# Latent attention in a two-block network: weight splits moved up, the query root finished on one engine, key roots by a power, rotary keys turned behind each latent norm

## The chip, the cores and the metric

The program runs on one core of a Trainium2 chip. The metric is the device time of one execution in microseconds (us): lower is better. The engines named below are TensorE (PE, with its weight loads as PEld), VectorE (DVE), ScalarE (ACT), GpSimd (POOL) and SyncE (SP), which here only issues transfers. Each runs its own instructions in order and meets the others at semaphores.

## The reference, cut to what matters

Two network blocks run one after the other on 256 tokens of width 1024. Their stages are called ffn0, mamba, ffn1, ffn2, mla and ffn3 (the first block), and conv and stick (the second). Only the latent attention (mla) is touched by the change:

```python
def mla_mixer(h, positions, w_in, q_a_norm, kv_a_norm, w_q_b, w_kv_b, q_norm, k_norm, w_out):
    proj = h @ w_in                                   # 1024 -> 384 + 256 + 32
    cq = rms_norm(proj[..., :384], q_a_norm)
    ckv = rms_norm(proj[..., 384:640], kv_a_norm)
    k_rope = proj[..., 640:]
    q = (cq @ w_q_b).reshape(b, s, 16, 96)            # 64 "nope" + 32 "rope" per head
    kv = (ckv @ w_kv_b).reshape(b, s, 16, 128)        # 64 key + 64 value per head
    ...
    q_nope, q_rope, k_nope, k_rope = (rms_norm of each, over its own last axis)
    q_rope = apply_rope(q_rope, cos, sin)
    k_rope = apply_rope(k_rope, cos, sin)
    o = causal_block_attention(q_nope, q_rope, k_nope, k_rope, v)
    return o.reshape(b, s, 1024) @ w_out
```

`rms_norm(x, w)` is `x * rsqrt(mean(x*x) + 1e-6) * w`.

## The kernel before, in words

**Products.** Every large product is done in fp32r as three matmuls (`product`, lines 559 to 561): high part times high part, high times low, low times high. So each weight unit (up to 2048 columns of 128 partitions, 1 MB) that lands in `raw` is split twice: ACT copies it, rounded, to `w_hi` (line 1173), and DVE subtracts to get `w_lo` (line 1668). Units go round a ring of four slots. SP may load unit u when `w_lo` of unit u-4 is done; ACT may split unit u when PE has used unit u-4; PE may use unit u when its `w_lo` is done.

**The order is written out by hand**, engine by engine. `split_to(n)` on ACT and on DVE means "split all units up to n, here in the queue". An engine's queue is in order, so whatever stands behind a split waits for it.

**The mla stage** has twelve weight units, called W0 to W11 here (`u0 + 0` to `u0 + 11` in the code): W0, W1 and the short W2 (128x1280) are the latent projection, W3 to W5 (128x1536) the query weights, W6 and W7 the key and value weights, W8 to W11 the output weights. There are two token blocks (tb 0 and 1) of 128 tokens. PE's order is: latent projection of both blocks; transposes of `proj`; query products for both blocks; key and value products for block 0, then for block 1 with the transposes of `q_tok` between them (two `token_turn("q", ...)` after each of four products); transposes of `k_tok` for block 0; scores of rounds 0 to 3; transposes of `k_tok` for block 1; and then, interleaved, the rounds 0 to 11 of softmax weights (`weights_turn`), values (`values`), scores and output products (`out_unit`, `out_part`).

**The norms of queries and keys.** For each block ACT squares (`square_q`, `square_k`), DVE sums and scales (`q_means`, `k_means`), ACT takes the root (`root`), DVE the reciprocal (`inverse`), POOL does one Newton step (`refine`: four small linked instructions, lines 2350 to 2353), and then DVE scales `q_tok` (`scale_q`, lines 1945 and 1948) or POOL scales the keys into `k_tok` (line 2372). POOL also rotates the query's rope part (`rotate`, lines 2334 to 2341: five instructions a block) and the one rope part of the keys (lines 2365 to 2367, between the two query blocks). POOL's norm of the latents takes its inverse root by a power: `lrs` (line 2319), 128x3; in the mamba stage the same form makes `grs` (line 2289), 128x4.

**Transposed tiles** alternate between two PSUM banks (`tr`), so a transpose waits until the one two before it has been read, by ACT (even quads) or by DVE (odd quads: `read_turn`).

## Time and profile before

| what | value |
|---|---|
| runs of before | 1408.57 us median of 3 (1407.95 to 1410.07) |
| the profiled execution | 1409.99 us, its span 1408.2 us |
| mean granted TensorE clock | 0.968 of full speed (full is 2.4 GHz, the lower level 1.2 GHz) |
| PE busy | 1327.6 us (94%) |
| DVE, ACT, POOL busy | 772.2 (55%), 673.6 (48%), 132.9 us (9%) |
| HBM traffic | 216.82 MB read, 155 GB/s over the span |

The span is the time from the first to the last instruction in the trace; the execution's own time is 1.8 us more. The mla stage begins at about 840 us of the span and its last output product ends at about 975 us. In the timeline a row gives start, duration, engine, line, operation and tiles, with the count of instructions merged, and in brackets how long the engine sat idle before it and what released it.

### The profile page before, as it was taken

The numbers are of one execution on the slowest core, as the hardware profiler recorded it, in microseconds if no ns is written. First come the engines' busy times: TensorE is split into PE (matmuls) and PEld (weight loads), VectorE is DVE, ScalarE is ACT, GpSimd is POOL, SyncE is SP. The second block draws the span as 40 slices with busy tenths as digits, with TensorE's granted clock in tenths as the row PEclk, the third lists the DMA queues.
The fourth block names the chain that finished last, engine by engine and source line by source line (L and its number), as shares of the span: only waits on it lengthen the run. The fifth ranks groups of instructions, "written<-read, shape, count | busy, mean of one in ns | idle before, by whom it ended". The sixth has DMA issues, their size and how long they took to land.

```text
span 1408.2 us, 18444 instructions
## 1 busy us (share of the span) xinstructions
PE 1327.6 (94%) x7004; PEld 1130.8 (80%) x7004; DVE 772.2 (55%) x918; ACT 673.6 (48%) x878; POOL 132.9 (9%) x224
## 2 busy tenths in 40 slices
PE   6999999998889999999999998789999998997977
PEld 5888878997668888888888887678888878996965
DVE  4655545778656555545555445555555545664552
ACT  5544446664546544435444437545554334434441
POOL 3000001036540000000000004500000000000000
PEclk9999999999889999999999999989999999998989
DMA  8665534552125555563655634041755664653301
GB/s 277 196 192 190 202 120 152 179 179 87 63 90 187 172 179 179 179 231 116 221 179 181 232 121 150 30 121 60 239 179 179 209 179 120 180 180 120 120 1 45
DMA packets 179726, 218.78 MB, mean 155 GB/s; under 512 B 8553, under 2 KB 132782, under 8 KB 179662
## 3 DMA queue, kind: packets, MB, share of 16 engines
q1 hardware_dynamic: 179374, 217.75, 47.7%
q8 instruction: 43, 0.70, 0.2%
q0 software_dynamic: 288, 0.15, 0.1%
q14 instruction: 21, 0.17, 0.0%
HBM read 216.82 MB, written 1.05 MB: 155 GB/s over the span
## 4 chain that ended last, share of the span: by engine, by line
PE 85%; DVE 6%; ACT 4%; issue 2%; POOL 2%; DMA 0%; SPq 0%; POOLq 0%; ACTq 0%; DVEq 0%
PE acc L559 26%; PE acc L561 25%; PE acc L560 25%; PE tr L576 3%; DVE w_lo L1668 2%; ACT w_hi L1173 1%; ACT xT_hi L1181 1%; PE tr L807 1%; PE aux L949 1%; DVE conv L1864 1%; DVE xT_lo L1677 1%; DVE E L1822 0%; DMA raw<-in_ffn_w_up 0%; PE aux L1065 0%; PE aux L1066 0%
## 5 line engine op out<-in xcount | busy, mean ns | idle before, releaser
L1668 DVE TENSOR_TENSOR w_lo<-raw,w_hi 128x2048 fp32r<-128x2048 f32 (+1 forms) x207 | 465.8, 2278 | 212.7 <-ACT w_hi L1173 212.7
L1173 ACT ACTIVATE w_hi<-raw 128x2048 fp32r<-128x2048 f32 (+1 forms) x207 | 385.5, 1901 | 135.5 <-PE acc L561 126.9
L559 PE MATMUL acc<-w_hi,xT_hi 128*128 128x512 f32 (+1 forms) x898 | 361.8, 403 | 19.1 <-DVE hT_lo L1677 8.0
L561 PE MATMUL acc<-w_hi,xT_lo 128*128 128x512 f32 (+1 forms) x898 | 354.1, 394 | 0.0
L560 PE MATMUL acc<-w_lo,xT_hi 128*128 128x512 f32 (+1 forms) x898 | 353.8, 394 | 0.0
L559 PEld LDWEIGHTS acc<-w_hi,xT_hi 128*128 128x128 f32 x898 | 173.4, 193 | 55.3 <-DVE hT_lo L1677 8.5
L561 PEld LDWEIGHTS acc<-w_hi,xT_lo 128*128 128x128 f32 x898 | 172.5, 192 | 36.6
L560 PEld LDWEIGHTS acc<-w_lo,xT_hi 128*128 128x128 f32 x898 | 173.6, 193 | 33.6
L559 PE MATMUL acc<-w_hi,hT_hi 128*128 128x512 f32 x448 | 176.4, 394 | 3.4 <-DVE hT_lo L1677 2.6
L560 PE MATMUL acc<-w_lo,hT_hi 128*128 128x512 f32 x448 | 175.1, 391 | 0.0
L561 PE MATMUL acc<-w_hi,hT_lo 128*128 128x512 f32 x448 | 175.1, 391 | 0.0
L559 PE MATMUL acc<-xT_hi,w_hi 128*128 128x256 f32 (+1 forms) x560 | 159.0, 285 | 5.0 <-DVE w_lo L1668 3.4
L560 PE MATMUL acc<-xT_lo,w_hi 128*128 128x256 f32 (+1 forms) x560 | 158.5, 283 | 0.0
L561 PE MATMUL acc<-xT_hi,w_lo 128*128 128x256 f32 (+1 forms) x560 | 158.4, 283 | 0.0
L1752 DVE SCALAR_TENSOR_TENSOR h<-acc,rstd,sg 128x256 f32<-128x256 f32 x88 | 38.5, 480 | 164.7 <-ACT sg L1242 164.7
L1242 ACT ACTIVATE sg<-acc,rstd 128x256 f32<-128x256 f32 x88 | 36.9, 471 | 180.7 <-PE acc L561 180.7
L559 PEld LDWEIGHTS acc<-xT_hi,w_hi 128*128 128x128 f32 (+1 forms) x560 | 107.2, 191 | 5.8 <-issue 3.6
L2244 POOL TENSOR_SCALAR mean_square<-square_sum 128x1 f32<-128x1 f32 x18 | 4.9, 272 | 1103.3 <-ACT junk L1203 1103.2
L560 PEld LDWEIGHTS acc<-xT_lo,w_hi 128*128 128x128 f32 (+1 forms) x560 | 107.3, 192 | 0.3
L561 PEld LDWEIGHTS acc<-xT_hi,w_lo 128*128 128x128 f32 (+1 forms) x560 | 107.2, 191 | 0.0
L559 PEld LDWEIGHTS acc<-w_hi,hT_hi 128*128 128x128 f32 x448 | 84.5, 189 | 21.6 <-issue 2.8
L561 PEld LDWEIGHTS acc<-w_hi,hT_lo 128*128 128x128 f32 x448 | 84.5, 189 | 17.8
(277 smaller groups left out, 1226.4 us busy)
## 6 DMA issues: line engine op xcount, KB each, us to landing
raw<-in_ffn_w_gate SPq DMA_DIRECT2D x88, 512.0 KB, 4.3
raw<-in_ffn_w_up SPq DMA_DIRECT2D x88, 512.0 KB, 5.5
raw<-in_ffn_w_down SPq DMA_DIRECT2D x88, 512.0 KB, 4.8
raw<-in_ssm_w_in SPq DMA_DIRECT2D x48, 512.0 KB, 4.7
raw<-in_w_in_a SPq DMA_DIRECT2D x64, 256.0 KB, 4.1
raw<-in_ssm_w_out SPq DMA_DIRECT2D x16, 512.0 KB, 4.3
...
```

The costliest lines, as they stand in the source:

```text
L559: pe.matmul(o, lh, rh, start=start, stop=False, skip_group_check=skip)
L560: pe.matmul(o, lh, rl, start=False, stop=False, skip_group_check=skip)
L561: return pe.matmul(o, ll, rh, start=False, stop=stop, skip_group_check=skip)
L576: last = pe.transpose(tr[0:n, k % 2, at:at + P], src, ident[:])
L807: last = pe.matmul(tr[:, k % 2, tb * GW + r * HP:tb * GW + (r + 1) * HP], E[:, tb, r * P:(r + 1) * P], xdt[:, g % 2, tb, r * HP:(r + 1) * ...
L949: last = pe.matmul(aux[:, r % 2, j * (VD + 1):(j + 1) * (VD + 1)], pT[:, r % 2, at:at + P], kv_tok[:, kb, h0 + j, NOPE:], start=kb == 0, s ...
L1173: act.activation(w_hi[:, u % RING, 0:n], raw[:, u % RING, 0:n], ACT.Copy).then_inc(hi_ready, 1)
L1181: inst = act.activation(dst, tr[:, k % 2, at:at + P], ACT.Copy, scale=scale)
L1242: act.activation(sg[:, tb, :], bank(p0 + n, tb)[:, 0:CW], ACT.Silu, scale=rstd[:, tb:tb + 1]).then_inc(gated, 1)
L1668: dve.tensor_tensor(w_lo[:, u % RING, 0:n], raw[:, u % RING, 0:n], w_hi[:, u % RING, 0:n].bitcast(F32), ALU.subtract).then_inc(lo_ready, 1)
L1677: inst = dve.scalar_tensor_tensor(dst, tr[:, k % 2, at:at + P], scale, hi.bitcast(F32), ALU.mult, ALU.subtract)
L1752: acc_free(dve.scalar_tensor_tensor(h[:, tb, :], bank(p0 + n, tb)[:, CW:2 * CW], rstd[:, tb:tb + 1], sg[:, tb, :], ALU.mult, ALU.mult), p0 ...
```

## The change

Five things change, all in the mla stage.

1. **Splits.** W2 is split on ACT between the two halves of the stage's input (behind block 0's eight rounded copies) and on DVE ahead of block 1's eight low parts. W8 is split on ACT ahead of `read_kv(0, 3)` and on DVE behind `read_kv(1, 1)`. W9 is split on ACT between two query tile reads and on DVE behind `tops(3)`. W10 and W11 are subtracted on DVE in two halves of 1024 columns (`split_half`), the first half of W10 ahead of `read_weights(5)` and the second behind it, the halves of W11 on either side of `tops(8)`. SP's order of loads is the same.
2. **Query root.** The Newton step on the query roots moves from POOL to DVE, right behind the reciprocal (five linked instructions in `inverse`); `scale_q(1)` now comes ahead of the read of query tile (0, 1).
3. **Key root.** ACT's root, DVE's reciprocal and POOL's four-instruction step give way to one power instruction, 128x16, on POOL for each block.
4. **Rotary keys.** They are rotated on POOL right behind each block's latent norm, in a tile of their own (`rot`), not between the two query rotations.
5. **The semaphores** `inverse_ready` and `q_rstd` go.

```diff
@@ layer_input, ACT and (below) DVE
                     input_high(tb)
+                    if c.name == "mla" and tb == 0:
+                        split_to(c.unit + 3)
...
+                if c.name == "mla":
+                    split_to(c.unit + 3)
                 input_low(c.name, 1)
@@ mla, ACT
                 read_kv(0, 2)
-                root("q", 1)
+                split_to(u0 + 9)
                 read_kv(0, 3)
+                root(1)
                 square_k(0)
                 read_kv(1, 0)
                 read_turn("q", 0, 0)
-                root("k", 0)
                 read_turn("q", 0, 2)
                 read_kv(1, 2)
                 read_turn("q", 1, 0)
+                split_to(u0 + 10)
                 read_turn("q", 1, 2)
                 square_k(1)
                 read_turn("k", 0, 0)
                 read_turn("k", 0, 2)
-                root("k", 1)
                 exps(0)
...
                 out_high(0)
-                split_to(u0 + 9)
                 read_weights(2)
...
                 exps(5)
-                split_to(u0 + 10)
                 out_high(2)
@@ DVE
+            def split_half(u, half):
+                at = slice(half * UNIT // 2, (half + 1) * UNIT // 2)
+                dve.wait_ge(hi_ready, u + 1)
+                inst = dve.tensor_tensor(w_lo[:, u % RING, at], raw[:, u % RING, at], w_hi[:, u % RING, at].bitcast(F32),
+                                         ALU.subtract)
+                if half:
+                    inst.then_inc(lo_ready, 1)
+                    c.split = u + 1
...
-                def inverse(kind, tb):
-                    rs = {"q": qrs, "k": krs}[kind][:, tb]
-                    dve.wait_ge(roots_ready, tb + 1 + (2 if kind == "k" else 0))
-                    dve.reciprocal(rs, rs).then_inc(inverse_ready, 1)
+                def inverse(tb):
+                    rs, ms, tmp = qrs[:, tb], qss[:, tb], newton[:]
+                    dve.wait_ge(roots_ready, tb + 1)
+                    link(dve.reciprocal(rs, rs))
+                    link(dve.tensor_tensor(tmp, rs, rs, ALU.mult))
+                    link(dve.tensor_tensor(tmp, tmp, ms, ALU.mult))
+                    link(dve.tensor_scalar(tmp, tmp, -0.5, 1.5, ALU.mult, ALU.add))
+                    link(dve.tensor_tensor(rs, rs, tmp, ALU.mult))
...
+                inverse(1)
+                scale_q(1)
                 read_turn("q", 0, 1)
                 k_means(0)
-                scale_q(1)
                 read_turn("q", 0, 3)
-                inverse("k", 0)
                 read_kv(1, 1)
+                split_to(u0 + 9)
                 read_turn("q", 1, 1)
...
                 tops(3)
+                split_to(u0 + 10)
                 read_turn("k", 1, 1)
...
-                split_to(u0 + 11)
+                split_half(u0 + 10, 0)
                 read_weights(5)
+                split_half(u0 + 10, 1)
                 tops(7)
                 out_norm(5)
-                split_to(u0 + 12)
+                split_half(u0 + 11, 0)
                 tops(8)
+                split_half(u0 + 11, 1)
@@ POOL, behind each latent norm
+                    x1, x2 = v[:, 0:HALF], v[:, HALF:]
+                    cs, sn = cos[:, tb, :], sin[:, tb, :]
+                    for n, (v, w) in enumerate(((x1, cs), (x2, sn), (x2, cs), (x1, sn))):
+                        inst = pool.tensor_tensor(rot[:, n, :], v, w, ALU.mult)
+                    link(inst)
+                    pool.tensor_tensor(x1, rot[:, 0, :], rot[:, 1, :], ALU.subtract)
+                    link(pool.tensor_tensor(x2, rot[:, 2, :], rot[:, 3, :], ALU.add))
...
                 for tb in range(TB):
                     rotate(tb)
-                    refine(qrs[:, tb], qss[:, tb], tb + 1).then_inc(q_rstd, 1)
...
                 for tb in range(TB):
-                    link(refine(krs[:, tb], kss[:, tb], tb + 3))
+                    pool.wait_ge(means_ready, tb + 3)
+                    link(pool.tensor_tensor(krs[:, tb], kss[:, tb], minus_half[:, 0:MH], ALU.pow))
                     pool.tensor_tensor(k_tok[:, tb, :, 0:NOPE], kv_tok[:, tb, :, 0:NOPE], ...
```

**Three places in the order of instructions.** DVE at the start of the stage, before: `x` is the residual, `xT_lo` the low parts of the input (one set of eight for each block), `w_lo` the splits.

```order
L1729 SCALAR_TENSOR_TENSOR x<-acc,x 128x512 x2
L1677 SCALAR_TENSOR_TENSOR xT_lo<-tr,cols,xT_hi 128x128 x8
L1729 SCALAR_TENSOR_TENSOR x<-acc,x 128x512 x2
L1677 SCALAR_TENSOR_TENSOR xT_lo<-tr,cols,xT_hi 128x128 x8
L1668 TENSOR_TENSOR w_lo<-raw,w_hi 128x1280
```

And the same place in the changed kernel (its line numbers are up to 15 higher):

```order
L1740 SCALAR_TENSOR_TENSOR x<-acc,x 128x512 x2
L1686 SCALAR_TENSOR_TENSOR xT_lo<-tr,cols,xT_hi 128x128 x8
L1740 SCALAR_TENSOR_TENSOR x<-acc,x 128x512 x2
L1667 TENSOR_TENSOR w_lo<-raw,w_hi 128x1280
L1686 SCALAR_TENSOR_TENSOR xT_lo<-tr,cols,xT_hi 128x128 x8
```

The split of W2 (128x1280) has moved ahead of block 1's low parts; ACT's has moved in the same way between its two sets of eight.

DVE in the middle of the stage, before, from the root of query block 0 to the reads of the query tiles (`qT`):

```order
L1940 RECIPROCAL qrs<-qrs 128x32
L1945 TENSOR_TENSOR q_tok<-q_tok,qrs 128x16x64
L1948 TENSOR_TENSOR q_tok<-q_tok,qrs 128x16x32
L1925 TENSOR_REDUCE qss<-squares 128x16
L1926 TENSOR_REDUCE qss<-squares 128x16
L1928 TENSOR_SCALAR qss<-qss 128x16 x2
L1940 RECIPROCAL qrs<-qrs 128x32
L1964 COPY qT<-tr 96x4x128
L1933 TENSOR_REDUCE kss<-squares 128x16
L1934 TENSOR_SCALAR kss<-kss 128x16
L1945 TENSOR_TENSOR q_tok<-q_tok,qrs 128x16x64
L1948 TENSOR_TENSOR q_tok<-q_tok,qrs 128x16x32
```

And the second block's part of it in the changed kernel:

```order
L1952 RECIPROCAL qrs<-qrs 128x32
L1953 TENSOR_TENSOR newton<-qrs 128x32
L1954 TENSOR_TENSOR newton<-newton,qss 128x32
L1955 TENSOR_SCALAR newton<-newton 128x32
L1956 TENSOR_TENSOR qrs<-qrs,newton 128x32
L1960 TENSOR_TENSOR q_tok<-q_tok,qrs 128x16x64
L1963 TENSOR_TENSOR q_tok<-q_tok,qrs 128x16x32
L1979 COPY qT<-tr 96x4x128
L1944 TENSOR_REDUCE kss<-squares 128x16
L1945 TENSOR_SCALAR kss<-kss 128x16
L1979 COPY qT<-tr 96x4x128
L1971 TENSOR_SCALAR kv_tok<-acc,lrs 128x4x128
```

The four Newton instructions stand behind each reciprocal (also the first block's), and the first read of a query tile has moved behind the second block's root and scaling.

POOL from the second query rotation to the keys in the changed kernel:

```order
L2356 TENSOR_TENSOR t<-q_tok,rope_a 128x512
L2357 TENSOR_TENSOR t<-q_tok,rope_b 128x16x16
L2359 TENSOR_TENSOR t<-q_tok,rope_b 128x16x16
L2362 TENSOR_TENSOR q_tok<-t 128x16x16
L2363 TENSOR_TENSOR q_tok<-t 128x16x16
L2371 COPY k_tok<-kr 128x16x32 x2
L2374 TENSOR_TENSOR krs<-kss,minus_half 128x16
L2375 TENSOR_TENSOR k_tok<-kv_tok,krs 128x16x64
L2374 TENSOR_TENSOR krs<-kss,minus_half 128x16
L2375 TENSOR_TENSOR k_tok<-kv_tok,krs 128x16x64
```

Here both query rotations follow each other with nothing between them; before, sixteen small instructions (a Newton step and the rotary keys) stood between them and four more behind the second, and each `krs` took four instructions.

## Rows read from the trace of the kernel before

**Rows 1.** The profile's page: the chain that ended last, by engine.
```profile
PE 85%; DVE 6%; ACT 4%; issue 2%; POOL 2%; DMA 0%; SPq 0%; POOLq 0%; ACTq 0%; DVEq 0%
```

**Rows 2.** Windows: length; PE, PEld, DVE, ACT, POOL busy; granted clock, DMA share, GB/s.
```profile
846.80:850.90 4.10, 0.03 (x1) 0.04 (x1) 1.77 (x3) 3.99 (x6) 3.27 (x6) 1.00 0.00 0
850.90:857.00 6.10, 6.10 (x26) 5.92 (x27) 1.63 (x1) 0.93 (x3) 2.54 (x7) 0.50 0.79 242
862.87:865.59 2.72, 2.72 (x26) 2.72 (x25) 1.02 (x2) 2.44 (x4) 0.00 (x0) 1.00 0.02 6
865.60:885.10 19.50, 19.50 (x91) 16.16 (x90) 13.86 (x17) 17.44 (x28) 12.54 (x19) 1.00 0.61 216
885.30:900.70 15.40, 9.65 (x51) 7.67 (x50) 9.16 (x16) 5.64 (x11) 12.24 (x25) 0.89 0.01 1
900.70:911.97 11.27, 9.40 (x73) 7.84 (x73) 6.57 (x11) 7.25 (x16) 2.78 (x5) 1.00 0.00 0
911.97:930.60 18.63, 14.88 (x75) 12.56 (x74) 10.41 (x17) 9.11 (x19) 0.00 (x0) 0.73 0.19 57
919.70:929.40 9.70, 8.19 (x29) 7.05 (x29) 5.48 (x11) 4.02 (x7) 0.00 (x0) 0.50 0.37 108
937.40:942.80 5.40, 4.04 (x17) 3.29 (x17) 3.16 (x6) 2.63 (x3) 0.00 (x0) 0.71 0.62 187
```

**Rows 3.** Timeline of all engines around the stage's first wait.
```profile
843.65 2.17 ACT L1181 ACTIVATE xT_hi<-tr,cols 128x128 fp32r<-128x128 f32 x8 [4.19 <-PE tr L576]
...
848.03 2.63 ACT L1173 ACTIVATE w_hi<-raw 128x1280 fp32r<-128x1280 f32 x2
...
849.32 3.22 DVE L1668 TENSOR_TENSOR w_lo<-raw,w_hi 128x1280 fp32r<-128x1280 f32 x2 [2.33 <-ACT w_hi L1173]
...
850.87 0.50 PE L559 MATMUL acc<-w_hi,xT_hi 128*128 128x160 f32 x1 [4.08 <-DVE w_lo L1668]
```

**Rows 4.** Timeline of DVE around the query norms.
```profile
877.10 0.84 DVE L1928 TENSOR_SCALAR qss<-qss 128x16 f32<-128x16 f32 x2
...
882.78 1.23 DVE L1945 TENSOR_TENSOR q_tok<-q_tok,qrs 128x1024 f32<-128x1024 f32 x1 [2.38 <-POOL qrs L2353]
883.92 0.71 DVE L1948 TENSOR_TENSOR q_tok<-q_tok,qrs 128x512 f32<-128x512 f32 x1
...
887.20 0.62 DVE L1964 COPY qT<-tr 96x512 f32<-96x512 f32 x1
...
894.43 1.10 DVE L1948 TENSOR_TENSOR q_tok<-q_tok,qrs 128x512 f32<-128x512 f32 x1
```

**Rows 5.** Timeline of POOL: the two rotations' first step, the second's last, keys.
```profile
873.76 2.75 POOL L2334 TENSOR_TENSOR t<-q_tok,rope_a 128x512 f32<-128x512 f32 x1 [2.83 <-ACT q_tok L1427]
...
887.78 1.26 POOL L2334 TENSOR_TENSOR t<-q_tok,rope_a 128x512 f32<-128x512 f32 x1
...
891.21 0.75 POOL L2341 TENSOR_TENSOR q_tok<-t 128x256 f32<-128x256 f32 x1
...
907.54 1.92 POOL L2372 TENSOR_TENSOR k_tok<-kv_tok,krs 128x1024 f32<-128x1024 f32 x1
```

**Rows 6.** Groups of POOL by shape: the powers of three and four elements.
```profile
L2289 POOL TENSOR_TENSOR grs<-gms,minus_half 128x4 f32<-128x4 f32 x4 | 4.0, 1012 | 0.3
...
L2319 POOL TENSOR_TENSOR lrs<-lms,minus_half 128x3 f32<-128x3 f32 x2 | 1.7, 858 | 0.2
```

**Rows 7.** Timeline of PE: three of its waits.
```profile
895.58 1.94 PE L576 MATMUL tr<-ident,q_tok 128*96 128x128 f32 x8 [3.20 <-DVE q_tok L1948]
...
918.39 1.31 PE L949 MATMUL aux<-kv_tok,pT 128*128 128x65 f32 x8 [1.34 <-ACT pT L1484]
921.21 0.66 PE L576 MATMUL tr<-ident,o_tok 128*128 128x128 f32 x2 [1.51 <-DVE xT_lo L1999]
```

**Rows 8.** Timeline around the split of W10: DVE, then PE.
```profile
935.87 2.29 DVE L1668 TENSOR_TENSOR w_lo<-raw,w_hi 128x2048 fp32r<-128x2048 f32 x1 [0.98 <-ACT w_hi L1173]
...
938.82 1.26 PE L949 MATMUL aux<-kv_tok,pT 128*128 128x65 f32 x8 [1.36 <-DVE pT L1982]
```

39 lines of the change are left out of this document (8 added, 31 removed).

## The prediction, as it was made before the changed kernel ran

> **What bounds the kernel now.** I read the chain that ended last first: TensorE holds 85% of it [rows 1], so a change pays where it takes away TensorE's waits, or the half clock that follows them. I then cut the mla stage into windows at its waits [rows 2], and looked up in the timelines which instruction ends each wait [rows 3 to 8]. Five stretches matter. From 846.8 to 850.9 PE does nothing, and from 850.9 to 857.0 it runs at a granted clock of 0.50, the 1.2 GHz level. From 865.6 to 885.1 it never stops. From 885.3 (first transposes of queries) to 900.7 (first transposes of keys) it is busy for 9.65 of 15.4 us. From 900.7 to 911.97 (first values) it is busy for 9.40 of 11.27 us. From 911.97 to 930.6 (weights of round 4 transposed) it is busy for 14.88 of 18.63 us, and the clock there is 0.73, because it is 0.50 from 919.7 to 929.4. I take the terms in this order. All times are those of before; a term says by how much PE reaches the end of its stretch earlier.
>
> **Term 1, W2 split early: 7.4 us.** PE waits 4.08 us for `w_lo` of W2 at 850.87 [rows 3]. Its two splits wait for nothing but their place: ACT does it at 848.03 behind block 1's copies and squares of x, DVE at 849.32. ACT is idle for 4.19 us ahead of 843.65 [rows 3], which is where its split now stands (about 1.2 us for 1280 columns: row of 2.63 us for 1280 and 1536 columns together), and the DVE one follows at about 841.8, behind the residual, done by 843.3. The slot is free: PE used W2's predecessor in it before it transposed block 0's input, which ACT's copies at 837 already needed. So PE goes on at 846.8 at full clock: the wait of 4.1 us goes, and of the 6.1 us at clock 0.50 [rows 2] half, 3.05 us, and another 0.3 us because the low level lasts to about 857.6. (As a check, the 24 matmuls of 160 columns take 2.72 us at clock 1.00 [rows 2]; they begin the stretch at 0.50 and take 5.2 us there.) PE arrives at 858.2, not at 865.6: 7.4 us earlier. Everything this needs on ACT and DVE (the reads of `proj`, W4, W5) follows PE and shifts with it; W3 is done by 851.4, for use at 858.2. The stretch to 885.1 has no wait and runs at clock 1.00 [rows 2], so it shifts whole, and W6's load now starts at 843, in a stretch where the DMA share is 0.00 [rows 2]. I see nothing that gives this back. Bounds: 4.1 (the wait alone, clock low anyway) to 7.5.
>
> **Term 2, query and key norms: 0, from -1.5 to +3.5.** Removed: POOL's Newton steps, the rotary keys between its rotations, ACT's and DVE's key roots. Query block 1 gains most: its rotation starts at 887.78 and its last step ends at 891.96 [rows 5], then a Newton step, and `scale_q(1)` ends at 895.53 [rows 4], for which PE waits 3.20 us [rows 7]. Added on DVE: four small instructions a block. DVE's cheapest of this kind take some 0.13 to 0.25 us, so 0.9 us for four; alone, block 0 would be scaled at 880.4 (the end of the reciprocal: `L1945` starts at 882.78 after 2.38 us idle) + 0.9 + 1.15 + 0.7 = 883.2, before PE wants it at 885.3.
>
> But they are not alone. POOL now has its whole rotation of block 1 to do in those microseconds, without a pause. The rows show that POOL and DVE stop each other: `L2334` took 2.75 us beside a split and a sum, and 1.26 us otherwise [rows 5]; `L1948` took 1.10 us beside a POOL copy and 0.71 us otherwise, and the two small `L1928` took 0.84 us together beside rotation steps [rows 4]. The Trainium skill, "SBUF — State Buffer", section "Who interferes with whom", says that a DVE instruction with two SBUF inputs and a GpSimd instruction that reads SBUF exclude each other for a whole instruction, whichever starts first. By that rule each Newton instruction waits out one rotation step; the trace agrees as far as the three rows go.
>
> If each of the Newton instructions lets one of POOL's steps (0.75 to 1.26 us) go first, `L1945` starts at about 885.0, waits once more before `L1948`, and block 0 is scaled at 887.7: PE, which has never waited there, waits 2.4 us. From there the first read of a query tile by DVE (887.20 today) comes behind block 1's means, root and reciprocal (today 887.20 - 884.63 = 2.6 us), Newton (0.9) and scaling (1.9): 893.1. PE's fourth query transposes can only go at 893.8 instead of 890.4, its fifth at 895.7. That is where they are today, since the 3.20 us wait for block 1 is gone. Behind it the keys: `k_means(0)` to 895.15, the power, and then `k_tok` (1.92 us [rows 5]). The power of 128x3 takes 0.858 us and that of 128x4 1.012 us [rows 6], 0.154 us per element; a line through both gives 1.012 + 12 x 0.154 = 2.86 us for 128x16 (lower bound 1.01, if the rest is free). It ends at 898.0, in W8's split on DVE (about 896.5 to 898.75), so `k_tok` is ready at 900.7: the time of today. Without the mutual stops the same chain gives 897.2, 3.5 us earlier. With them and a half clock in the waits I count 1.5 us later. I take 0, since the rows speak for the stops.
>
> **Term 3, second key block and W9: -2.0, from +0.85 to -3.3.** Today the keys of block 1 are scaled at 909.46 (907.54 + 1.92 [rows 5]), 8.75 us after the first key transposes. Their means are ready 4.8 us after those, today and then. The power ends at 7.7, `k_tok` at 9.7 if it starts ahead of W9's split on DVE, which now stands behind `tops(3)` at 7.9. The split then runs to 12.0, and the transposed tile (1, 1) is read behind it; values begin at 13.3 instead of 11.27. If the split goes first, `k_tok` is ready at 12.1, values at 14.6: -3.3. With a power of 1.01 us it is +0.85. The table load ahead of the exponentials no longer waits for a key root, which is worth up to 0.4 us here and lies inside the wait.
>
> **Term 4, W8 and W9 gone from the softmax: 4.3, from 2.2 to 6.3.** Between 911.97 and 930.6 PE waits 1.34 us for a `pT` that ACT reads behind W8's copy and 1.51 us for an `xT_lo` behind DVE's half of it [rows 7]. Both go (2.85 us); a new wait of 0.65 us for the `pT` of round 3 comes up behind the low part of the first output tile and its norm. That is 2.2 us. PE is busy for 8.19 us at clock 0.50 [rows 2]; at full clock this is 4.1 us less. But PE comes to this stretch from a longer wait than today (term 3), so I give it back half: 2.2 + 2.1 = 4.3.
>
> **Term 5, W10 and W11 in halves: 1.3, from 0 to 2.3.** PE waits 1.36 us for `pT` of round 5 behind W10's 2.29 us split [rows 8]. With half of it in front, the wait is about 0.3 us. The clock of 0.71 in the 5.4 us around it [rows 2] costs 4.04 x 0.29 = 1.2 us more. PE then meets ACT's unchanged split of W11 ahead of `pT` of round 6, and waits for it about 1 us: 1.1 + 1.2 - 1.0 = 1.3.
>
> **Sum.** 7.4 + 0 - 2.0 + 4.3 + 1.3 = 11.0 us. Against the profiled execution (1409.99 us, span 1408.2): 1399.0 us and a span of 1397.2. That execution is 1.4 us above the median of before, 1408.57, from which the sum gives 1397.6. I say 1397.5.
>
> **Rivals.**
> - *A, 11 us as above, within 1392.5 to 1402.5 (0.62).*
> - *B, the engines don't stop each other (0.15).* If POOL's steps slip in without holding DVE, term 2 is +3.5, and with the full clock terms 4 and 5 are 6.3 and 2.3: 7.4 + 3.5 - 2.0 + 6.3 + 2.3 = 17.5, so 1391. For it: block 1's wait of 3.20 us is the largest left, and the shorter POOL queue takes aim at it. Against it: the three rows on stops.
> - *C, only W2 pays (0.18).* The waits taken from the softmax come back ahead of the first values: term 2 -1.5, term 3 -3.3, terms 4 and 5 at their lower ends 2.2 and 0: 7.4 - 1.5 - 3.3 + 2.2 = 4.8, so 1403.8. For it: three waits in a row with little work between them leave the clock low, as 0.50 from 850.9 and from 919.7 show [rows 2].
> - *D, slower (0.03).* The power stands on the path twice. For the change to be slower by over 2.8 us it must lose 13.8 us against the sum, 6.9 for each power: one of 128x16 would have to take 9.8 us, not 2.86. The two sizes on record lie on a line, so a jump that large is unlikely; from about 8.4 us on it would eat the whole gain.
> - *The change does not do what it says (0.02).* If something else holds W2 (its data, its slot), term 1 is 0 and 1405 is left. But SP had no load open in that stretch (DMA share 0.00 [rows 2]).
>
> **How the numbers follow.** 0.2% of this kernel is 2.8 us; a difference below that is no difference here. The likeliest case gives 1397.5. A reaches 1392.5 to 1402.5; to leave out no more than 2 in 10, I add B's side down to 1389 and most of C up to 1403.5. The sign hangs on D and the last case alone: faster 0.95, within 0.2% 0.03, slower 0.02.
>
> **What the profile after would show.** Term 1: no idle ahead of the matmuls of 160 columns, and clock 1.00 through 865. Term 2: the four Newton instructions of block 0 take 0.2 us each if I am wrong on the stops, 0.7 us and more if right; PE waits some 2 us ahead of the first query transposes. Term 3: the power of 128x16 at 2.9 us, a wait of PE of 2 us or more for the second `k_tok`. Term 4: no wait of PE behind W8 or W9, and the clock of the stretch above 0.73. Term 5: a wait below 0.5 us at round 5, and one of 1 us at round 6. I am wrong if the clock falls in the stretch to 885.1, if the power is far from the line, or if a full clock returns all through the softmax (then B).

## The result, and the profile after

The changed kernel took 1424.18 us (median of 20 executions, 1407.47 to 1427.71). The kernel before, on the same chip, took 1409.58 us (median of 20, 1405.70 to 1411.62). The ratio is 1.0083, with a 95% interval from 1.0064 to 1.0101 (1.0104 by the medians): slower, where 1397.5 us and a gain were forecast. The executions of the changed kernel fall into three groups: three near 1408 us, six from 1415 to 1419 and eleven from 1423 to 1428. Those of before lie within 6 us. All medians here and below are taken over all executions of a run, its slowest group among them.

To see where the time went I cut both traces at POOL's `mean_square`, which begins each stage. The first fence is the kernel before, the second the changed one. The stretches are ffn1, mla, ffn3 and stick; columns as in [rows 2].

```profile
472.84:659.89 187.05, 186.97 (x854) 154.54 (x853) 97.44 (x87) 82.75 (x86) 1.50 (x5) 1.00 0.57 185
846.95:979.70 132.75, 115.42 (x621) 96.98 (x622) 74.14 (x123) 70.39 (x134) 35.49 (x67) 0.91 0.30 96
979.70:1156.58 176.88, 176.88 (x802) 146.11 (x801) 92.04 (x69) 84.96 (x75) 1.50 (x5) 1.00 0.61 194
1290.71:1397.57 106.86, 95.35 (x556) 79.96 (x555) 45.16 (x62) 42.70 (x54) 1.66 (x6) 0.89 0.13 45
```
```profile
476.39:665.13 188.74, 188.64 (x854) 154.55 (x853) 97.41 (x87) 82.92 (x86) 1.50 (x4) 1.00 0.56 184
853.88:977.18 123.30, 111.86 (x620) 93.23 (x619) 76.17 (x130) 68.83 (x131) 36.98 (x52) 0.93 0.30 98
977.18:1155.68 178.50, 178.50 (x802) 146.02 (x801) 92.05 (x69) 85.09 (x75) 1.50 (x5) 1.00 0.60 193
1290.58:1415.39 124.81, 113.17 (x555) 90.62 (x554) 45.16 (x62) 42.75 (x54) 1.66 (x6) 0.74 0.11 39
```

The mla stage, the only one that the change is about, is 9.45 us shorter (132.75 to 123.30). Two things happen in stages whose code is untouched. ffn1 and ffn3 are 1.69 and 1.62 us longer, with the same number of instructions, hardly any wait and full clock; all stages but mla and stick together lose 9.3 us (6.93 ahead of mla, 2.39 between mla and stick). And the stick stage is 17.95 us longer at a mean clock of 0.74 instead of 0.89. 9.3 + 17.95 - 9.45 = 17.8 us is the whole difference of the two spans (1426.0 and 1408.2; the profiled execution of the changed kernel is its slowest, 1427.71 us).

**The untouched ffn stages.** Groups of PE by shape: a product with `hT_hi` held and 512 columns of `w_lo` passing takes 391 ns in the kernel before and 397 ns in the changed one, 6 ns more on each of 448 (and of two more such groups). The same with `xT_hi` held is unchanged. First before, then after:

```profile
L560 PE MATMUL acc<-w_lo,xT_hi 128*128 128x512 f32 x882 | 348.3, 395 | 0.0
L560 PE MATMUL acc<-w_lo,hT_hi 128*128 128x512 f32 x448 | 175.1, 391 | 0.0
```
```profile
L560 PE MATMUL acc<-w_lo,xT_hi 128*128 128x512 f32 x882 | 347.4, 394 | 0.0
L560 PE MATMUL acc<-w_lo,hT_hi 128*128 128x512 f32 x448 | 177.8, 397 | 0.0
```

The change allocates `newton` (128 bytes a partition) and `rot` (256) ahead of `pos_i`, so everything behind them (a few small tiles, hT, and the buffers of the later stages) lies 384 bytes further on; `raw`, `w_hi`, `w_lo`, x and xT stay. That is the only thing about hT that the change touches. The description of the change ahead of the prediction says that all of it is in the mla stage, and its diff leaves the two allocations out: they move addresses in every stage.

**The stick stage.** PE waits there for DVE's `zn`, 7.49 us before and 7.62 us after, and the clock falls in that wait. The first product behind it, before and then after:

```profile
1356.48 1.19 PE L1065 MATMUL aux<-s_qT,s_kT 64*128 64x256 f32 x2 [7.49 <-DVE zn L2129]
```
```profile
1355.85 1.19 PE L1065 MATMUL aux<-s_qT,s_kT 64*128 64x256 f32 x2 [7.62 <-DVE zn L2144]
```

Windows from the fall on, before and then after:

```profile
1352.80:1366.30 13.50, 9.82 (x28) 7.05 (x28) 7.96 (x11) 7.30 (x6) 0.00 (x0) 0.50 0.01 1
1366.50:1389.00 22.50, 22.50 (x116) 15.71 (x116) 2.55 (x6) 4.35 (x10) 0.00 (x0) 1.00 0.00 0
```
```profile
1352.40:1366.00 13.60, 10.15 (x29) 7.17 (x30) 7.74 (x11) 7.33 (x7) 0.00 (x0) 0.50 0.00 1
1366.00:1389.00 23.00, 23.00 (x62) 14.79 (x63) 1.70 (x4) 2.55 (x6) 0.00 (x0) 0.50 0.00 0
1389.00:1406.90 17.90, 17.90 (x55) 12.13 (x53) 0.85 (x2) 1.78 (x4) 0.00 (x0) 0.50 0.00 0
```

Before, the clock is back at 1.00 from 1366.3 and PE does 116 products in 22.5 us. After, PE is busy without a gap and the clock nevertheless stays at the 1.2 GHz level until 1407.0; PE does 62 products in 23 us. Below I call the first an early return, the second a late one. Where an execution has no trace, I tell the two by its time and its mean clock (0.97 or more in the early groups, 0.95 to 0.96 in the late ones).

**The mla stage** answers to [rows 2] so (ends of the stretches at the same instructions: products of 160 columns done, first transposes of queries, first of keys, first values, weights of round 4):

```profile
850.90:857.00 6.10, 6.10 (x41) 5.49 (x40) 2.69 (x9) 5.99 (x15) 2.36 (x7) 1.00 0.58 172
862.20:864.92 2.72, 2.72 (x26) 2.72 (x25) 1.02 (x2) 2.44 (x4) 1.05 (x6) 1.00 0.32 127
864.93:885.10 20.17, 19.84 (x91) 16.12 (x89) 16.74 (x21) 19.61 (x30) 14.88 (x21) 1.00 0.58 209
885.20:898.45 13.25, 9.82 (x50) 7.71 (x51) 11.93 (x20) 6.65 (x11) 7.46 (x6) 0.87 0.07 15
898.45:914.05 15.60, 10.85 (x73) 9.18 (x74) 8.68 (x11) 7.50 (x16) 6.87 (x2) 0.83 0.38 123
914.05:929.48 15.43, 14.14 (x74) 12.15 (x74) 7.03 (x16) 5.32 (x17) 0.00 (x0) 0.73 0.01 2
```

Timelines of PE, POOL and DVE at the new wait for the second block's keys, which is 4.32 us:

```profile
910.32 3.93 PE L576 MATMUL tr<-ident,k_tok 128*96 128x128 f32 x16 [4.32 <-POOL k_tok L2375]
```
```profile
903.32 2.90 POOL L2374 TENSOR_TENSOR krs<-kss,minus_half 128x16 f32<-128x16 f32 x1 [5.54 <-DVE kss L1945]
906.30 3.97 POOL L2375 TENSOR_TENSOR k_tok<-kv_tok,krs 128x1024 f32<-128x1024 f32 x1
```
```profile
880.15 0.68 DVE L1954 TENSOR_TENSOR newton<-newton,qss 128x32 f32<-128x32 f32 x1
...
881.08 1.18 DVE L1956 TENSOR_TENSOR qrs<-qrs,newton 128x32 f32<-128x32 f32 x1
...
888.12 0.19 DVE L1954 TENSOR_TENSOR newton<-newton,qss 128x32 f32<-128x32 f32 x1
...
888.57 0.19 DVE L1956 TENSOR_TENSOR qrs<-qrs,newton 128x32 f32<-128x32 f32 x1
...
906.21 2.28 DVE L1667 TENSOR_TENSOR w_lo<-raw,w_hi 128x2048 fp32r<-128x2048 f32 x1
```

### The profile page after: what moved, and what is told of

The parts are those of the page before. It is cut to its first block, busy times and chain, and to the rows that moved or that the text cites. A ratio compares the mean times of both kernels' runs of the same rounds, so it can differ in the third digit from the quotient of the medians.

```text
span 1426.0 us, 18436 instructions
## 1 busy us (share of the span) xinstructions
PE 1352.5 (95%) x7004; PEld 1139.7 (80%) x7004; DVE 775.7 (54%) x926; ACT 674.4 (47%) x876; POOL 134.9 (9%) x210
## 3 DMA queue, kind: packets, MB, share of 16 engines
HBM read 216.82 MB, written 1.05 MB: 153 GB/s over the span
## 4 chain that ended last, share of the span: by engine, by line
PE 86%; DVE 7%; ACT 4%; issue 1%; POOL 1%; DMA 0%; SPq 0%; POOLq 0%; ACTq 0%; DVEq 0%
PE acc L559 25%; PE acc L561 25%; PE acc L560 25%; PE tr L576 3%; DVE w_lo L1667 2%; ACT w_hi L1173 1%; PE tr L807 1%; ACT xT_hi L1181 1%; PE aux L949 1%; PE aux L1065 1%; PE aux L1066 1%; DVE conv L1875 1%; DVE xT_lo L1686 1%; PE acc L1124 1%; DMA raw<-in_ffn_w_up 0%
## 5 line engine op out<-in xcount | busy, mean ns | idle before, releaser
L559 PE MATMUL acc<-w_hi,hT_hi 128*128 128x512 f32 x448 | 179.4, 400 | 3.3 <-DVE hT_lo L1686 2.6
```

The source lines that it names most:

```text
L559: pe.matmul(o, lh, rh, start=start, stop=False, skip_group_check=skip)
```

## The experiments

My theory had two parts. Placement: hT's new address makes its products slower. Instant: what keeps the clock low in the stick stage is when PE's wait falls against the clock's own changes, so that a shift of tenths of a us in otherwise untouched code can flip it. The rival for both was that changed instructions are the cause, and for the clock that the addresses of the stick stage's buffers, which moved too, keep it low. Some executions fall into groups, so I give the groups beside the medians.

### Where the new buffers lie

**tiles_last:** the two allocations moved behind `region_g`.
```
-        newton = sb("newton", [P, 2, MH])
-        rot = sb("rot", [P, 4, HALF])
...
         sb("region_g", [P, 9024])
+        newton = sb("newton", [P, 2, MH])
+        rot = sb("rot", [P, 4, HALF])
```


> The changed kernel with its two new buffers (newton, 128 bytes a partition, and rot, 256 bytes) allocated behind region_g, so that hT and everything behind it lies where it lay before the change; nothing else differs. Placement theory (the 384 bytes by which hT moved make its products slower): the products with hT_hi and hT_lo held take 389 ns again and not 395, each ffn stage is 1.65 us shorter than in the changed kernel, and the stick stage starts near 1281.2 us of the trace (1290.7 less the 9.45 that the mla stage gained). Rival (the products are slower for another reason, the changed program's length or the chip it ran on): 395 ns stay and the stick stage starts near 1290.6. The end then depends on the stick stage's clock. If the late return of the clock also comes from the placement: near 1400 us, with all executions within some 4 us. If it comes from the instant at which PE's wait falls: executions stay in groups some 8 us apart, between 1400 and 1418 us.

**before_pad384:** the kernel before, with `sb("pad", [P, 96])` ahead of `pos_i`, unused.

> The kernel before with one unused buffer of 384 bytes a partition ahead of pos_i, and not one instruction changed. Placement theory: the products with hT held take 395 ns, not 389, each ffn stage is about 1.65 us longer, the stick stage starts near 1300.0 us (1290.7 + 9.3), and the run takes 1419 us if the stick stage stays as before. Rival (it is the changed instructions): 389 ns, 1409.6 us. On the stick stage's clock: if the placement is what keeps it low, this kernel too spends some 17 us more there (1436 us) in more than half of its executions; if the instant of the wait is what counts, its executions fall in groups of their own, not those of the changed kernel.

Measured, same chip: 1416.44 us (four executions from 1398.2 to 1400.8, seven from 1415.5 to 1419.2, and one of 4596.8 that nothing here explains) and 1436.57 us (five from 1433.9 to 1437.7), against 1410.29 for before (which had one execution of 1906.6 us). The expectations' 389 and 395 ns are means inside an ffn stage; over the whole program, as in the fences here, they are 391 and 397. Stage windows of the first (ffn1, mla, stick), then the product group of each:

```profile
472.68:659.70 187.02, 186.94 (x854) 154.53 (x853) 97.42 (x87) 82.75 (x86) 1.49 (x4) 1.00 0.57 185
846.76:967.76 121.00, 108.72 (x620) 90.84 (x619) 76.63 (x130) 68.67 (x131) 36.87 (x53) 0.96 0.30 99
1279.40:1405.32 125.92, 114.41 (x556) 91.72 (x555) 45.16 (x62) 42.70 (x54) 1.66 (x6) 0.74 0.11 38
```
```profile
L560 PE MATMUL acc<-w_lo,hT_hi 128*128 128x512 f32 x448 | 175.1, 391 | 0.0
```
```profile
L561 PE MATMUL acc<-w_lo,hT_hi 128*128 128x512 f32 x448 | 177.8, 397 | 0.0
```

The placement theory holds from both sides: with the buffers last the whole change costs nothing outside mla as far as the stick stage (391 ns, ffn1 187.02 us, stick reached at 1279.4, 11.3 us earlier than before), and 384 unused bytes in the untouched kernel bring 397 ns and put the stick stage's start at 1299.74, 9.0 us late. On the clock they split: `tiles_last` has hT and the stick buffers where they were and still returns late in most executions, so the placement is not needed for that; `before_pad384` returned late in all five, which is what I had expected for the case that the placement does keep the clock low.

**ffn_offsets** and **front128:** hT at another place in each ffn stage; in the second `raw`, the weights, x and xT moved by 128 bytes as well. `region_h`, which holds hT, grows to make room, so what lies behind it moves too.
```
+        hT_of = [overlaid((f"_s{f}", [P, n], F32), (f"hT{f}_hi", ...), (f"hT{f}_lo", ...))[1:]
+                 for f, n in enumerate((96, 32, 64, 128))]       # front128: (64, 32, 16, 48)
```


> The kernel before, with hT at another place in each ffn stage: moved by 384 bytes in ffn0, 128 in ffn1, 256 in ffn2 and 512 in ffn3 (hT of the other stages unmoved, everything behind region_h moved by 512). Placement theory: 395 ns in ffn0 for the products with hT_hi held, as in the changed kernel; the other three tell whether the moved distance or the address that it leads to counts. If only the address 147456 (144 x 1024, where hT begins in the changed kernel) is bad, ffn1, ffn2 and ffn3 stay at 389 ns and the time is 1.65 us over the kernel before; if any move does it, all four are slower and it is 6.6 us. Rival (not the place of hT but that of the buffers behind it): all four at 395 or all four at 389 whatever their place.

> The kernel before with an unused buffer of 128 bytes ahead of raw, so that raw, w_hi, w_lo, x and xT begin at multiples of 256 bytes and not 128 beyond one, and with hT at another place in each ffn stage: 0 beyond a multiple of 256 in ffn0, 128 in ffn1, 64 in ffn2, 192 in ffn3. In the kernel before every one of these buffers lay 128 beyond; hT at 0 beyond was slow (395 ns), at 128 fast (389 ns), wherever else it lay. If the address of hT alone counts: ffn1 as fast as before (about 187.1 us from mark to mark), ffn0 1.6 us slower than 170.8. If it is hT's place against that of w that counts: ffn0 fast and ffn1 slow. 64 and 192 beyond are open.

Stage windows ffn0 to ffn3, `ffn_offsets` and then `front128` (one execution each, 1411.47 and 1412.61 us):
```profile
27.02:199.07 172.05, 172.05 (x776) 141.34 (x775) 89.83 (x83) 80.01 (x77) 2.95 (x5) 1.00 0.57 190
470.84:659.34 188.50, 188.41 (x854) 154.75 (x853) 97.44 (x87) 82.76 (x86) 1.50 (x5) 1.00 0.56 184
659.34:846.38 187.04, 186.79 (x852) 154.08 (x850) 97.42 (x87) 82.78 (x86) 1.48 (x5) 1.00 0.55 179
980.81:1157.66 176.85, 176.85 (x802) 146.09 (x801) 92.04 (x69) 84.95 (x75) 1.50 (x4) 1.00 0.61 194
```
```profile
25.93:196.75 170.82, 170.82 (x776) 141.23 (x775) 89.85 (x83) 80.10 (x77) 2.96 (x5) 1.00 0.57 192
471.94:660.41 188.47, 188.38 (x854) 154.75 (x853) 97.45 (x87) 82.83 (x86) 1.50 (x5) 1.00 0.54 184
660.41:849.16 188.75, 188.48 (x852) 154.13 (x850) 97.46 (x87) 82.88 (x86) 1.49 (x5) 1.00 0.52 177
982.29:1159.67 177.38, 177.38 (x802) 146.08 (x801) 92.05 (x69) 85.00 (x75) 1.51 (x4) 1.00 0.58 194
```
The kernel before has 170.80, 187.05, 187.06 and 176.88. hT moved by 384 or 128 bytes costs 1.3 to 1.5 us a stage (394 ns a product), moved by 256 or 512 nothing (389 ns; one execution each). In `front128` the address that was slow is fast and the one that was fast is slow, because w moved: what counts is the distance of hT from w, both 128 beyond a multiple of 256 bytes in the kernel before. (`raw`, x and xT moved together with `w_hi` and `w_lo`; that it is w rather than one of them is argued from these products' reading only w and hT, and no run separates them.) With the distance at 0 beyond such a multiple: fast; at 128 or 64: slow (394 and 395 ns); at 192 in between, 0.5 us on the stage, with 388, 392 and 395 ns in its three groups where 0 has 389, 389 and 390 to 392. The theory "a bad address" falls, that of a bad distance stands.

**after_pad128:** the changed kernel with `sb("pad", [P, 32])` behind `rot`: 512 bytes in all.

> The changed kernel with one more unused buffer of 128 bytes behind newton and rot, so that hT lies 512 bytes from its place in the kernel before, not 384: its distance from w is a multiple of 256 bytes again. Theory: the products with hT held take 389 ns and not 395 in all four ffn stages, as with 256 and 512 in the run that moved hT by stage, and the stick stage starts near 1280, though the buffers stay where the change puts them. Rival (only the very place of before is fast, or the 2 new buffers themselves cost): 395 ns, 1290.6.

391 ns, ffn1 187.07 us, stick reached at 1279.47: as expected, with the new buffers where the change puts them. (1417.89 us in its one execution, a late return.)

### When the clock returns in the stick stage

**last_warm:** 28 unused products on PE ahead of `weights(0)`.
```
+                claim(p0, 0)
+                for _ in range(28):
+                    pe.matmul(bank(p0, 0), xT_hi[:, 0, 0:P], xT_hi[:, 0:2, :], start=True, stop=True)
                 weights(0)
```


> The kernel with the new buffers last, and 28 more products (xT_hi 128x128 with xT_hi 128x512, 0.23 us each, into an accumulator that the heads' values overwrite later) ahead of the stick stage's weights(0), where PE waits 7.5 us for DVE's zn. They compute nothing that is used. If the stick stage's low clock comes from PE's standing idle in that wait: the granted clock stays 1.00 behind it, the stretch from 1356.5 to 1366.4 of the kernel before, 9.9 us at 0.50, takes about 5 us less, the executions lie within some 4 us, and the median is near 1395 us (1409.6 less 9.5 for mla less 5). Rival (the small products of the stick stage keep the clock low by themselves): the clock falls to 0.50 there anyway, and the times are those of the kernel with the buffers last.

1398.20 us: nine executions from 1394.9 to 1402.5, three near 1415. Both expectations are half right. The clock did not fall in the filled wait, and the lower group is some 2 us below that of `tiles_last` (medians 1397.6 and 1399.9); but in the profiled execution, one of the three near 1415, it fell later, at 1354.5, among the stage's own small products, and stayed low. Windows from the end of the wait:
```profile
1345.50:1354.70 9.20, 7.09 (x35) 4.86 (x35) 4.79 (x5) 7.14 (x7) 0.00 (x0) 0.99 0.00 0
1354.90:1395.60 40.70, 40.70 (x116) 27.53 (x117) 3.40 (x8) 4.27 (x10) 0.00 (x0) 0.50 0.03 12
```
So the wait is one way into the low clock, not the only one.

**last_plus2** and **before_plus13:** 2 and 13 unused products ahead of the last four heads of logits.

> The kernel with the new buffers last, and 2 more products (128x128 held, 128x512 through, 0.23 us each, result unused and overwritten) ahead of the stick stage's last four heads of logits, so that PE and all that follows it come 0.46 us later to the stick stage's weights(0). Theory of the instant: what decides is how far the fall of the clock in PE's wait stands ahead of the first product of zr with from_. In the traces with the early return that was 4.87 us (before) and 4.82 (hT moved by stage), in those with the late one 4.57 (changed kernel), 4.63 (buffers last) and 4.51 (unused buffer). With 0.46 us more it becomes about 5.1: the clock returns some 9 us behind that product in nearly all executions, and they lie together near 1400.5 us (1399.9, the lower group of the kernel with the buffers last, + 0.5), where that kernel had two thirds of its executions near 1416.6. Rival (something else in the changed program or its addresses keeps the clock low): two groups as before, median near 1417.

> The kernel before with 13 such products at the same place, 2.96 us. Nothing of the change is in it and no buffer has moved. Theory of the instant: PE's wait moves by 2.96 us, the fall of the clock moves by another amount, and I expect it at about 4.4 us ahead of the first product of zr with from_, on the side of the late return: the clock stays at 0.50 for some 50 us, the stick stage takes 17 to 19 us more, and the executions lie near 1410.3 + 3.0 + 17 = 1430 us. Rival (the time is the 13 products' alone): 1413.3 us, with the executions within some 4 us as before.

1416.79 us (one execution at 1398.7, five from 1416.1 to 1420.8) and 1409.29 us (five from 1406.5 to 1412.5, one at 1428.5; the kernel before had one at 1428.6 beside them). Both expectations fail, for a reason that the traces show: the products stood in the wait's shadow. DVE's chain starts from the first four heads, so with the 13 products PE waited 4.5 us instead of 7.5, and the end of the wait, counted from the start of the stage, did not move (65.75 us, 65.77 before). They tested nothing but this: 3 us of work on PE cost nothing there. That the kernel before itself has an execution at 1428.6 matters too (and one at 1429.7 beside the next runs): now and then it takes as long as with a late return, with no change at all.

**last_delay2, before_delay13, before_delay6:** the same ahead of the first four heads, so that DVE's chain and the end of the wait move too. Two of the expectations give the distance as its excess over a fixed part of it; the distances themselves are in the table below.
```
+                        if n == 3 and half == 0:
+                            acc_done(pe, c.pair - 1, 0)
+                            for i in range(2):                   # 14, the last of 256 columns; 6
+                                pe.matmul(bank(c.pair + 1, 0), xT_hi[:, 0, 0:P], xT_hi[:, 0:2, :], ...)
```


> The kernel with the new buffers last and 2 products (128x128 held, 128x512 through, 0.23 us each, unused) ahead of the stick stage's first four heads of logits, from which DVE's zn follows: this moves the end of PE's wait as well (the 2 products ahead of the last four heads didn't: there the first product of zr with from_ came at the same distance from the stage's start). Theory of the instant: 1.22 us was this distance's excess over the clock's steps in the late trace of the kernel with the buffers last (1.10 and 1.16 in the other two late ones), 1.40 to 1.52 in those that returned early; with 0.46 more it is 1.68, and the clock returns early in nearly all executions, near 1400.5 us. Rival (the two groups come from something that such a shift doesn't touch): groups near 1400.5 and 1417, most in the upper one, as without the products (7 of 11).

> The kernel before with 13 such products and one of half the columns, 3.08 us, at the same place ahead of the first four heads of logits. No buffer has moved and nothing of the change is in it. Theory of the instant: this puts the end of PE's wait, against the steps of the clock, where it was in the three late traces (1.46 + 3.08 is 1.13 beyond the next step; they had 1.10, 1.16 and 1.22), so most executions spend some 17 us more at the clock of 0.50: near 1430 us. Rival (it is not the instant): 1413.5 us, executions within some 4 us, with one in ten or fewer near 1430.

> The kernel before with 6 products of 0.23 us, 1.37 us, at the place where 13 and a half (3.08 us) put all five executions at 1431 to 1434 us. Theory of the instant: 1.37 us leads to another place in the clock's steps, on the side of the early return, and the time is that of the products alone: 1411.5 us, at most one or two executions near 1431. Rival (any added work there keeps the clock low): all or most near 1430.

1401.20 us (ten from 1397.1 to 1402.7, two near 1416.5); 1432.28 us (all five from 1431.1 to 1433.8); 1423.27 us (all five from 1422.7 to 1424.9). Stick stage windows of the last two:
```profile
1291.12:1419.31 128.19, 116.92 (x570) 93.84 (x569) 45.24 (x62) 42.70 (x54) 1.65 (x5) 0.75 0.11 38
```
```profile
1291.07:1410.90 119.83, 108.57 (x562) 88.24 (x561) 45.23 (x62) 42.69 (x54) 1.65 (x5) 0.78 0.11 40
```
In a kernel with nothing of the change and no buffer moved, 3.08 us of products cost 22.8 us, and 1.37 us cost 13.8. The products' time alone does not explain either, and changed instructions or addresses are not needed for a late return. Whether addresses add to it is another question, and stays open (below). But `before_delay6` also breaks my expectation of it: I had it on the side of the early return. It has a middle case, a return 35 us behind the first product of `zr` with `from_`, which costs 12.4 us besides the products' own time. The changed kernel's middle group lies 8 us above its lowest; there is no trace of it, so whether it is the same case is not shown.

**after_delay2** and **w9_old_delay2:** the 2 products in the changed kernel, and in a later version (below).

> The changed kernel itself, buffers where it has them, with the 2 products ahead of the stick stage's first logits. If the instant of the wait is all that keeps its clock low, most executions move to its lowest group, 1407.5 to 1409.2 us, plus 0.5: median near 1409, against 1424.2 without them. Of the changed kernel's 15 us over the kernel before, some 15 are then the clock, and the 9 to 10 us of hT's products and the 9.5 to 12 us that the mla stage gained cancel. Rival (the address of the zn, zr and s_ buffers, which moved with hT, matters for the clock as well): the median stays above 1420.

> The kernel with the new buffers last and DVE's split of W9 at its old place, and the 2 products ahead of the stick stage's first logits. Theory of the instant: the clock returns early in nearly all executions, near 1395.3 us (1394.6, the lower group without the products, + 0.5 to 0.7), 1% below the kernel before, with 10 of 12 or more in that group. Rival (the products helped by luck): half of the executions near 1418.

1425.09 us (three from 1402.7 to 1408.0, nine from 1423.4 to 1428.3) and 1414.33 us (five from 1395.0 to 1401.0, seven from 1414.0 to 1419.4). Both expectations fail: 0.46 us is no lever; what it seemed to do in `last_delay2` it did in one kernel of three, and there it may be chance. For the changed kernel it is the rival's forecast that came true (a median above 1420): that the addresses of the stick stage's buffers, which moved with hT, help to keep its clock low is not excluded. What sorts the traces after the fact is how far the clock's fall stands ahead of the first product of `zr` with `from_`. The last column is the time at clock 0.50. (The expectations above have some of the distances up to 0.13 us smaller; these are read again, all in the same way. `last_warm` is left out, since its clock did not fall in the wait.)
```
return  distance, us               kernels                                         us at 0.50
early   4.83 to 4.96               before, ffn_offsets, front128, w2_only,         13.7
                                   keys_plain, w9_old_delay2
early   5.17                       keys_in_steps                                   20.5
early   6.42; 3.20, 2.96; 1.56     w9_behind; last_delay2, last_plus2;             10.2; 6.8; 10.2
                                   before_plus13
middle  6.08                       before_delay6                                   41.0
late    4.37, 4.57 to 4.73         before_delay13; after, after_pad128,            54.6
                                   before_pad384, after_delay2, tiles_last, w9_old
```
All seven late ones lie between 4.37 and 4.73 us, none of the eleven early ones does. This fits the theory of the instant and does not show it: it is one trace a kernel, the nearest early one is only 0.10 us away, the range was drawn after the traces were seen, and of the seven forecasts made from the theory two came true, those of `last_delay2` and `before_delay13` (two of the other five did not test it, since their products stood in the wait's shadow).

### The terms inside the mla stage

**w2_only:** the kernel before with the two `split_to(c.unit + 3)` of `layer_input` alone.

> The kernel before with the first part of the change alone: W2 of the mla stage split early on ScalarE and VectorE. Term 1 of the prediction: the wait of 4.1 us and the half clock behind it go, the stretch from 865.6 on comes 7.4 to 7.6 us earlier, the mla stage takes 125.2 us, not 132.75, and the stick stage starts near 1283.2. If the executions keep the early return of the clock in the stick stage: 1402.8 us (1410.3 - 7.5). By the theory of the instant the last part is open: some executions may lie 17 us higher, near 1420. Rival (the gain of the first wait comes back as a wait for queries or keys, which POOL sets, within the stage): mla above 128 us, total above 1405.5 in the lower group too.

1402.10 us, all four from 1401.1 to 1404.3, ratio 0.9934 (0.9888 to 0.9980). mla takes 125.60 us, 7.15 less than before; stick 106.95 (106.86 before). The rival falls.

**w9_behind** (one execution) and **w9_old:** `tiles_last` with DVE's split of W9 behind the second block's key tiles, and where it was before the change.
```
                 tops(3)
-                split_to(u0 + 10)
                 read_turn("k", 1, 1)
                 read_turn("k", 1, 3)
+                split_to(u0 + 10)            # w9_behind; w9_old has it behind tops(5)
```


> The kernel with the new buffers last, and DVE's split of W9 moved back by two instructions, from behind tops(3) to behind its two reads of the second block's key tiles. It tells what of the wait ahead of the second key transposes (4.32 us, with k_tok on POOL taking 3.97 us beside that split) is the split's and what is the power's. If DVE and POOL stop each other, k_tok takes 1.9 to 2.75 us, PE's wait shrinks by 1.2 to 2 us, and the first values begin 1.5 to 4 us earlier, counted from the first key transposes (the split of 2.3 us no longer stands ahead of the read of a key tile). Rival (the power alone sets it): the wait stays at 4.3 us and k_tok at 3.97.

> The kernel with the new buffers last, and DVE's split of W9 back where it stood before the change, behind tops(5). With it behind the two key tiles, k_tok took 1.91 us and not 3.97 and PE's wait for it 2.26 us and not 4.32, but PE then waited 2.69 us for the weights pT of round 1 that DVE read behind the split, so that the values of round 1 came only 0.9 us earlier. Here that wait goes: the values of rounds 0 and 1 come 2.5 to 3 us earlier than with the buffers last, counted from the first key transposes; the split costs again up to 1.5 us (the xT_lo of round 4's neighbourhood). I expect the mla stage at 119.5 us where the kernel with the buffers last had 121.0 and 123.9 in two traces, and the lower group of executions near 1398.5. Rival (the split is in somebody's way wherever it stands): the mla stage at 121 to 124 us.

Timelines of PE and POOL in `w9_behind`:
```profile
903.58 3.54 PE L576 MATMUL tr<-ident,k_tok 128*96 128x128 f32 x16 [2.26 <-POOL k_tok L2375]
911.31 0.48 PE L949 MATMUL aux<-kv_tok,pT 128*128 128x65 f32 x1 [2.69 <-DVE pT L1997]
```
```profile
898.63 2.90 POOL L2374 TENSOR_TENSOR krs<-kss,minus_half 128x16 f32<-128x16 f32 x1 [5.55 <-DVE kss L1945]
901.61 1.91 POOL L2375 TENSOR_TENSOR k_tok<-kv_tok,krs 128x1024 f32<-128x1024 f32 x1
```
Without the split beside it `k_tok` takes 1.91 us instead of 3.97 and PE waits 2.26 us instead of 4.32: 2.06 us of the wait were the split's, and the power is left. In `w9_behind` they came back at once as a wait of 2.69 us for the weights of round 1 that DVE reads behind the split, and its mla stage took 124.01 us. In `w9_old` that wait is 0.89 us; mla takes 118.30 us, and the executions lie at 1393.0 to 1395.2 (three) and near 1418 (two).

**keys_in_steps** and **keys_plain:** `w9_old` with the key roots back on three engines, with and without the 2 products.
```
-                    pool.wait_ge(means_ready, tb + 3)
-                    link(pool.tensor_tensor(krs[:, tb], kss[:, tb], minus_half[:, 0:MH], ALU.pow))
+                    link(refine(krs[:, tb], kss[:, tb], tb + 1))   # behind root on ACT, reciprocal on DVE
```


> As w9_old_delay2, but the key roots in the steps of the kernel before (root on ScalarE, reciprocal on VectorE, four small instructions on GpSimd) in place of the power of 128x16. The power takes 2.9 us from the means to k_tok; the steps on the three engines took so little that PE waited 0.57 us for the second block's keys in the kernel with W2 alone, against 2.26 us with the power. If the power is what is left of that wait, it shrinks to 0.6 us, the values come 1.7 us earlier, the mla stage is 1.5 to 2 us shorter, and the median 1.5 to 2 us below that of w9_old_delay2. Rival (the root's wait on ScalarE, with its table, and the reciprocal on VectorE cost as much elsewhere): the same time within 0.5 us, or more.

> The version with the key roots in steps, DVE's split of W9 at its old place and the new buffers last, without the 2 unused products in the stick stage. With them 10 of 11 executions lay between 1392.0 and 1398.8 us. If the products had no part in that: the same, median near 1394.5 us. If they had: a part of the executions, up to a half, near 1412 to 1418 us.

1394.98 us (ten from 1392.0 to 1398.8, one at 1412.4) and 1392.27 us (all five from 1390.7 to 1395.0; ratio 0.9887, 0.9868 to 0.9906). PE's wait for the second block's keys in `keys_in_steps`, and the mla and stick windows of `keys_plain`:
```profile
898.47 1.08 PE L577 MATMUL tr<-ident,k_tok 128*96 128x128 f32 x8 [0.58 <-POOL k_tok L2400]
```
```profile
844.66:961.00 116.34, 106.75 (x620) 88.91 (x619) 76.58 (x132) 69.05 (x133) 32.76 (x58) 0.99 0.31 104
1273.28:1378.24 104.96, 93.45 (x556) 78.61 (x555) 45.15 (x62) 42.72 (x54) 1.65 (x5) 0.91 0.13 46
```
The power was what was left: the wait goes from 2.27 us (`w9_old_delay2`) to 0.58, mla from 120.61 to 115.84. That is more than the 1.5 to 2 us expected, since the clock in the stage is 0.99, where it was 0.94; against `w9_old`, with the same instructions in mla at a mean clock of 0.97, it is 2.5 us. `keys_plain` is the best version, 17 us below the kernel before, without the unused products.

## Why the prediction was wrong, step by step

**The sum for the stage was near; the time was not the stage's.** Forecast: 11.0 us less. Measured in mla: 9.45 us in the changed kernel's trace, 11.75, 11.98 and 12.25 in `tiles_last`, `after_pad128` and `after_delay2`, which have the same instructions there, and 8.8 and 9.0 in `last_plus2` and `last_warm`. The spread comes with the clock in the stage, 0.93 to 0.96. That the sum is near is in part luck: terms 2, 3 and 4 are off by +1.6, -2.3 and -1.1 us.

- *Term 1, forecast 7.4:* 7.6 (PE arrives 11.04 us behind the stage's start, at 864.92, and not 18.64). Clock 1.00 throughout, as forecast; `w2_only` shows that it stands alone.
- *Term 2, forecast 0:* +1.6 (33.5 us from there to the first key transposes, 35.1 before). The mutual stops are there: of the Newton instructions of block 0, beside POOL's rotation, two took 0.68 and 1.18 us; in block 1, without it, 0.19 each. But the forecast let all four wait: the first took 0.35 us (0.19 in block 1), and the third, which reads one tile and not two, 0.18 in both blocks. The two scalings behind them were held too (1.70 and 1.24 us, 1.23 and 0.68 in block 1). The wait for the first queries is 0.43 us (1.05 in `tiles_last`), not 2.4. Here I had weighed the rule of the Trainium skill, "SBUF — State Buffer", section "Who interferes with whom"; the trace agrees with it where the two engines met.
- *Term 3, forecast -2.0, lower end -3.3:* -4.3. The power took 2.90 us (2.86 forecast). W9's split began at 906.21 and ran undisturbed in 2.28 us, and `k_tok`, 0.09 us behind it, took 3.97 us. That is the case of the lower end, "if the split goes first", and not the one that the sum took: `k_tok` was ready 11.8 us behind the first key transposes (12.1 forecast there). What no case had priced is the clock: it fell at 908.7, in the wait for `k_tok`, and from 910.32 to the first values PE took 3.7 us where it took 2.5 before at full clock.
- *Term 4, forecast 4.3:* 3.2, in the lower half of its bounds. PE's idle time fell by 2.5 us (2.2 forecast), its busy time by 0.7, where I had 2.1 for the clock; the clock of the stretch is 0.73, as before, so I gave back too little. *Term 5, forecast 1.3:* 1.4, with waits of 0.32 us at round 5 and 0.47 at round 6 (0.3 and 1 forecast).

**The step that failed** is one that the prediction does not write down: that everything outside the mla stage stays. It rests on the sentence "I see nothing that gives this back" and on a sum that is subtracted from the whole execution. The runs showed 9.3 us more in stages whose code is untouched and 17.95 us more in the stick stage, 27.25 us against the 9.45 that mla gave. Two things were left out.

*The two new buffers.* The full diff shows them ahead of `pos_i`; I read them as 384 bytes of scratch. They changed the distance between hT and w, and that costs 9.0 us in a kernel without the change (`before_pad384`), about all that mla gains in the changed kernel's trace. This is shown from both sides, and in the changed kernel itself (`after_pad128`). With an early return the changed kernel is no faster than the one before: its lowest three executions lie at 1407.5 to 1409.2 us.

*The clock of a later stage.* I treated a stage that is untouched and begins at the same time as unchanged. That its stretch at clock 0.50 can last 13.7, 41.0 or 54.6 us in kernels that differ by a few unused products is shown by `before_delay6` and `before_delay13`. That a late return costs the changed kernel's slowest executions some 18 us is read from its trace (54.6 us at 0.50, 124.81 us in the stage). Why it returns late there in 17 of 20 executions above 1415 us, eleven of them above 1423, is not shown: the instant fits (4.57 us), the moved addresses are a rival that no run rules out, and `before_plus13` is the control for `before_delay13`: as much work that does not move the end of the wait does nothing. Open is also what sets the distance in an execution, since a shift of 0.46 us went with an early return of most executions in one kernel and with no change to speak of in two; and why `before_pad384` returned late each time. I also cannot say what would keep the clock up there; `last_warm` shows that filling the wait alone does not.

*The rivals.* D, slower through a power of 128x16, did not happen, though the sign came out as D's; C's mechanism (the gain comes back ahead of the first values) happened in part, -4.3 in term 3. Of the signs that were to show the steps right, those of terms 1 and 3 came, and the wait at round 5; the wait of 2 us for the first queries, a clock above 0.73 behind W8 and W9 and the wait of 1 us at round 6 did not. The chance of 0.02 for slower came from mechanisms of mla alone.
